# Heads in pairs through scores and values in the stick-breaking attention of a two-block transformer kernel

## The reference, cut to what matters

```python
def stick_breaking_attention(q, k, v):
    for each block of 128 queries, for each of 8 heads:
        z = einsum('bhqd,bhkd->bhqk', q_blk, k) * dh ** -0.5        # dh = 64
        earlier = key_pos < query_pos
        log_keep = where(earlier, log_sigmoid(-z), 0)
        log_stick = cumsum(log_keep, axis=3, reverse=True) - log_keep
        w = where(earlier, exp(log_sigmoid(z) + log_stick), 0)
        out = einsum('bhqk,bhkd->bhqd', w, v)
```

## Time and profile before

| | us |
|---|---|
| median of 3 executions | 2090.99 |
| lowest, highest | 2090.92, 2093.43 |
| the profiled execution, its own time | 2092.2 |
| its span, first to last instruction | 2090.4 |

### The profile page before, as it was taken

The page is one execution under the profiler, slowest core; times in us unless marked ns, Lnnn a source line. Parts: engine busy times, 40 slices in busy tenths (PEclk is TensorE's granted clock), DMA queues, the critical chain, the costliest instruction groups (busy, mean ns, idle before and its releaser), DMA issues.

```text
span 2090.4 us, 28150 instructions
## 1 busy us (share of the span) xinstructions
PE 2043.1 (98%) x11092; PEld 1720.4 (82%) x11092; DVE 1374.6 (66%) x2469; ACT 1103.8 (53%) x1722; POOL 25.9 (1%) x51
## 2 busy tenths in 40 slices
PE   7999999998989999999999999999999999999998
PEld 5988899987767788888897888888888897788886
DVE  4445566656785557655696888656765697788653
ACT  4344455445444445654645666544655645666542
POOL 0000000000000000000000000000000000000000
PEclk9999999999999999999999999999999999999999
DMA  9785576664355856655533357554756533357551
GB/s 338 249 292 197 186 262 198 211 220 158 104 162 190 262 172 196 217 179 204 193 123 120 121 195 237 182 181 151 239 174 211 186 129 121 121 181 244 185 181 46
DMA packets 281763, 392.94 MB, mean 188 GB/s; under 512 B 9580, under 2 KB 175900, under 8 KB 281504
## 3 DMA queue, kind: packets, MB, share of 16 engines
q1 hardware_dynamic: 277472, 379.62, 55.4%
q0 software_dynamic: 3184, 9.04, 1.3%
q10 hardware_dynamic: 976, 2.49, 0.3%
HBM read 390.06 MB, written 1.05 MB: 187 GB/s over the span
## 4 chain that ended last, share of the span: by engine, by line
PE 64%; DVE 7%; issue 3%; ACT 3%; DMA 0%; POOL 0%; DVEq 0%; ACTq 0%; POOLq 0%
PE bank L815 17%; PE bank L817 17%; PE bank L816 17%; PE bank L779 9%; DVE junk L2633 2%; DVE wlo L1974 2%; PE bank L940 1%; DVE wlo L1969 1%; PE bank L863 1%; ACT whi L1387 1%; DVE tm L2789 0%; DVE stats L2044 0%; DVE x L2205 0%; ACT whi L1382 0%; ACT junk L1442 0%
## 5 line engine op out<-in xcount | busy, mean ns | idle before, releaser
L1969 DVE TENSOR_TENSOR wlo<-raw,whi 128x1024 fp32r<-128x1024 f32 x360 | 434.1, 1223 | 319.4 <-ACT whi L1382 317.8
L1382 ACT ACTIVATE whi<-raw 128x1024 fp32r<-128x1024 f32 x360 | 375.1, 1057 | 410.3 <-PE bank L817 211.1
L815 PE MATMUL bank<-whi,xTh 128*128 128x512 f32 (+1 forms) x1344 | 530.1, 394 | 6.9 <-issue 2.6
L817 PE MATMUL bank<-whi,xTl 128*128 128x512 f32 (+1 forms) x1344 | 521.3, 388 | 0.0
L816 PE MATMUL bank<-wlo,xTh 128*128 128x512 f32 (+1 forms) x1344 | 520.9, 388 | 0.0
L1974 DVE SCALAR_TENSOR_TENSOR wlo<-raw,cols,whi 128x512 fp32r<-128x512 f32 (+2 forms) x608 | 407.0, 721 | 134.0 <-ACT whi L1387 130.3
L1387 ACT ACTIVATE whi<-raw,cols 128x512 fp32r<-128x512 f32 (+2 forms) x608 | 385.6, 696 | 146.0 <-PE bank L817 107.3
L815 PEld LDWEIGHTS bank<-whi,xTh 128*128 128x128 f32 x1344 | 253.3, 188 | 62.0 <-issue 7.2
L817 PEld LDWEIGHTS bank<-whi,xTl 128*128 128x128 f32 x1344 | 252.9, 188 | 52.8
L816 PEld LDWEIGHTS bank<-wlo,xTh 128*128 128x128 f32 x1344 | 253.4, 189 | 48.7
L779 PE MATMUL bank<-xTh,whi 128*128 128x256 f32 x696 | 198.1, 285 | 0.2 <-DVE wlo L1969 0.2
(11 more groups left out here) (360 smaller groups left out, 2500.8 us busy)
## 6 DMA issues: line engine op xcount, KB each, us to landing
raw<-in_w_in SPq DMA_DIRECT2D x68, 1024.0 KB, 5.2
raw<-in_ffn_w_in SPq DMA_DIRECT2D x132, 512.0 KB, 6.1
raw<-in_ffn_w_gate SPq DMA_DIRECT2D x88, 512.0 KB, 4.2
raw<-in_ffn_w_up SPq DMA_DIRECT2D x88, 512.0 KB, 5.2
raw<-in_ffn_w_down SPq DMA_DIRECT2D x40, 1024.0 KB, 5.0
raw<-in_w_mod SPq DMA_DIRECT2D x36, 1024.0 KB, 6.6
raw<-in_ffn_w_out SPq DMA_DIRECT2D x30, 1024.0 KB, 5.1
raw<-in_w_out SPq DMA_DIRECT2D x12, 1024.0 KB, 5.0
```

Of the source, the lines that this page charges most:

```text
L815: e.matmul(o, hi[:, kc, sl], wh[:, c], start=at == 0 and k == 0, stop=False)
L817: ins = e.matmul(o, lo[:, kc, sl], wh[:, c], start=False, stop=fin)
L1382: e.activation(wh, raw, ACT.Copy).then_inc(m.whi_done, 1)
L1969: e.tensor_tensor(wl, raw, wh.bitcast(F32), ALU.subtract).then_inc(m.wlo_done, 1)
```

## The change

Scores and values take two heads at a time. `scores(p)` issues the four score matmuls of heads 2p and 2p+1, alternating between the row halves, into two banks, then the masks of both; `values(p)` issues the four value matmuls of the pair, alternating between the column halves. On PE the scores of a pair come in the even steps 0, 2, 4, 6 and the values of a pair in the odd steps 3, 5, 7, 9; `sticks` stays one head per step. ACT and DVE keep their order of one head per step. `ex` gets a third buffer, and head h uses buffer h mod 3. ACT's wait before a new head's absolute value is counted in pairs of values. The bank tables are not touched.

```diff
--- before.py
+++ after.py
@@ -660,7 +660,7 @@
         self.kT, o = self.at(o, "kT", [128, 4, 256])
         self.sv, o = self.at(o, "sv", [128, 2, 512])
         self.spl, o = self.at(o, "spl", [128, 2, 384])
-        self.ex, o = self.at(o, "ex", [128, 2, 384])
+        self.ex, o = self.at(o, "ex", [128, 3, 384])
         self.lam, o = self.at(o, "lam", [128, 8])
         self.la, o = self.at(self.b1_at, "la", [128, 2, 256])
         self.l1, o = self.at(o, "l1", [128, 2, 256])
@@ -1191,19 +1191,22 @@
         ins.then_inc(full, 1)
         step = [0]
 
-        def values(h):
-            hp, off, r = h // 2, (h % 2) * 64, h % 2
-            pr = slice(off, off + 64)
-            self.evacuated("sc", l, h)
-            if h % 4 == 0:
-                self.bank("bo", l, h // 4)
-                if h == 0:
+        def values(p):
+
+            pair = (2 * p, 2 * p + 1)
+            for h in pair:
+                self.evacuated("sc", l, h)
+            if p % 2 == 0:
+                self.bank("bo", l, p // 2)
+                if p == 0:
                     self.evacuated("sv", l, 1)
-            b = self.t.bank["bo", l, h // 4][0]
-            bank, cs, hc = m.psum[b], (hp % 2) * 256, slice(h * 64, h * 64 + 64)
-            self.mm(bank[pr, cs:cs + 256], m.sv[:, 0, hc], m.ex[:, r, 0:256], h % 4 < 2, False)
-            ins = self.mm(bank[pr, cs + 128:cs + 256], m.sv[:, 1, hc], m.ex[:, r, 256:384], False, h % 4 >= 2)
-            ins.then_inc(m.full[b] if h % 4 == 3 else m.value_mm, 1)
+            b = self.t.bank["bo", l, p // 2][0]
+            bank, cs = m.psum[b], (p % 2) * 256
+            for i, o, x in ((0, slice(cs, cs + 256), slice(0, 256)), (1, slice(cs + 128, cs + 256), slice(256, 384))):
+                for h in pair:
+                    pr = slice(h % 2 * 64, h % 2 * 64 + 64)
+                    ins = self.mm(bank[pr, o], m.sv[:, i, h * 64:h * 64 + 64], m.ex[:, h % 3, x], p % 2 == 0 and i == 0, p % 2 == 1 and i == 1)
+            ins.then_inc(m.full[b] if p % 2 else m.value_mm, 1)
 
         def sticks(h):
             r = h % 2
@@ -1214,26 +1217,28 @@
             self.mm(bank[:, 128:256], NO, m.spl[:, r, 256:384], False, False)
             self.mm(bank[:, 256:384], NL, m.spl[:, r, 256:384], False, True).then_inc(m.stick_mm, 1)
 
-        def scores(h):
-            hp, off = h // 2, (h % 2) * 64
-            pr = slice(off, off + 64)
-            if h == 0:
+        def scores(p):
+
+            if p == 0:
                 self.evacuated("sk", l, 1)
-            bank, full = self.bank("sc", l, h)
-            self.mm(bank[:, 0:256], m.kT[pr, hp, 0:128], m.qT[pr, hp, 0:256], True, False)
-            self.mm(bank[:, 256:384], m.kT[pr, hp, 128:256], m.qT[pr, hp, 128:256], False, False)
-            self.mm(bank[:, 0:128], m.ident[:, :], m.stk[:, 0:128], False, False)
-            self.mm(bank[:, 256:384], m.ident[:, :], m.stk[:, 0:128], False, False).then_inc(full, 1)
+            banks = [self.bank("sc", l, 2 * p + r) for r in range(2)]
+            for o, k, q in ((slice(0, 256), slice(0, 128), slice(0, 256)), (slice(256, 384), slice(128, 256), slice(128, 256))):
+                for r in range(2):
+                    pr = slice(64 * r, 64 * r + 64)
+                    self.mm(banks[r][0][:, o], m.kT[pr, p, k], m.qT[pr, p, q], o.start == 0, False)
+            for bank, full in banks:
+                self.mm(bank[:, 0:128], m.ident[:, :], m.stk[:, 0:128], False, False)
+                self.mm(bank[:, 256:384], m.ident[:, :], m.stk[:, 0:128], False, False).then_inc(full, 1)
 
         def each():
             n = step[0]
             step[0] += 1
-            if 2 <= n < 10:
-                values(n - 2)
+            if n % 2 and 3 <= n < 10:
+                values((n - 3) // 2)
             if 1 <= n < 9:
                 sticks(n - 1)
-            if n < 8:
-                scores(n)
+            if n % 2 == 0 and n < 8:
+                scores(n // 2)
 
         def decays():
             e.wait_ge(m.la_done, l + 1)
@@ -1831,15 +1836,15 @@
         def sticks(h):
             e.wait_ge(m.stick_mm, 8 * l + h + 1)
             b, n = self.t.bank["sc", l, h]
-            e.activation(m.ex[:, h % 2, :], m.psum[b][:, 0:384], ACT.Exp).then_inc(m.free[b], 1)
+            e.activation(m.ex[:, h % 3, :], m.psum[b][:, 0:384], ACT.Exp).then_inc(m.free[b], 1)
 
         def scores(h):
             bank, _ = self.filled("sc", l, h)
-            x = m.ex[:, h % 2, :]
-            if h == 5:
+            x = m.ex[:, h % 3, :]
+            if h in (5, 6):
                 self.filled("bo", l, 0)
-            elif h >= 2:
-                e.wait_ge(m.value_mm, 6 * l + h - 1 - (h - 2 >= 4))
+            elif h >= 3:
+                e.wait_ge(m.value_mm, 2 * l + (1 if h < 5 else 2))
             e.activation(x, bank[:, 0:384], ACT.Abs).then_inc(m.act, 1)
             self.own()
             e.activation(x, x, ACT.Exp, scale=-1.0).then_inc(m.act, 1)
@@ -2679,7 +2684,7 @@
             e.wait_ge(m.ln_done, 8 * l + h + 1)
             if h >= 2:
                 e.wait_ge(m.stick_mm, 8 * l + h - 1)
-            e.scalar_tensor_tensor(out=m.spl[:, h % 2, :], in0=bank[:, 0:384], scalar=0.0, in1=m.ex[:, h % 2, :],
+            e.scalar_tensor_tensor(out=m.spl[:, h % 2, :], in0=bank[:, 0:384], scalar=0.0, in1=m.ex[:, h % 3, :],
                                    op0=ALU.max, op1=ALU.add).then_inc(m.spl_done, 1)
 
         def each():
```

## The result

The changed kernel takes 2078.39 us (median of 4, 2076.09 to 2081.99) beside 2090.95 (2089.15 to 2093.43) for the kernel before: ratio 0.9942, 95% interval 0.993 to 0.9955. That is 12.6 us faster, inside the range 2077.0 to 2088.0. The forecast of 2082.6 gave 8.4 of the 12.6. The profiled execution took 2076.09, its span is 2074.2 instead of 2090.4.

A forecast was written before the change was run, and what follows sets the result against it. PE, busy for 98% of the span, was taken to bound the kernel. Saving 4.5 us per mixer up to softplus 5, 9.0 for both, gave 2083.2 or 2082.0 by scale, middle 2082.6 us; range 2077 to 2088.

The forecast's parts named there:

- Overlap of the halves: PE's pairs on opposite array halves stream together: scores 0.85 us, values 0.81; the rival without overlap, 2087.8 us, had chance 0.09.
- The rival with 0.05: Only scores overlap; the two pairs of values lose 0.65 us each, giving 2085.2 us; chance 0.05.
- Step 0: Scores 0 and 1 put about 0.5 us more before the first stall, which shrinks from 3.49 to 3.0; no cost.
- Step 1: After sticks 0 at low clock, the sub comes earlier; sticks 1 start at about 1124.55 instead of 1126.72.
- the clock does not fall: Rival: clock stays up in first stalls, 2.75 us less a mixer; one 2079.9 us, both 2077.1; chance 0.17.
- Steps 2 to 5: From sticks 1 on, steps of 6.62, 5.51 and 8.14 us, then softplus 5 at 1148.16, 4.5 us earlier.
- Steps 6 and 7: DVE's distances from softplus 5 stay fixed: softplus 6 after 7.01 us, sticks 7 after 14.11; PE early at sticks 6 by 0.4.
- the new stall: PE waits 2.7 us for DVE in front of sticks 7; all that PE saves in steps 6 and 7 goes there.
- The clock behind it: Granted clock after sticks 7 stays 1.00; rival: it falls, 3.3 us a mixer; one 2085.9 (chance 0.13), both 2089.2 (0.07).
- The stall of 2.18 us that stood as harmless: Stall at 610.99 us, followed by a clock of 1.00; taken as a length that did not bring the clock down.
- Sum: 4.5 us saved per mixer, 9.0 for both mixers.
- The midpoint between two scales: 2082.6 us, the middle between 2083.2 (from the profiled execution's 2092.2) and 2082.0 (in the scale of the median 2090.99).

The follow-up runs named there:

- e6: Changed kernel with ACT's and DVE's work on the decays moved behind the scores of head 1: 2072.23 us, ratio 0.9908 to the kernel before.
- e8: Kernel before with one edit on PE, head 1's scores issued in step 0 behind head 0's, unpaired: 2082.10 us, ratio 0.9957.
- e5: Changed kernel with DVE's softplus ahead of the tap in steps 6 and 7, step 7's last two chunk states after softplus: 2070.89 us, ratio 0.99.
- e1: Changed kernel with one head's matmuls issued before the other's within each pair, no alternation: 2077.23 us, ratio 0.9936 to the kernel before.
- e3: Changed kernel with only values in pairs, scores and their step as in the kernel before: 2084.41 us, ratio 0.997 to the kernel before.
- e4: Kernel before with the third buffer of ex and ACT's wait moved back one head, nothing paired: 2090.59 us, ratio 0.9996.
- r_after: The changed kernel measured again, unedited, beside the kernel before: 2078.87 us, ratio 0.9938.

## Why the prediction was right, step by step

- **Overlap of the halves**: right. 0.85 and 0.80 for pairs, forecast 0.85 and 0.81. The chunk states pointed the right way, although their two groups lie on different row halves, so that they were no pure case of shared rows; the values' pair is one. The rival with 0.05, which the Trainium skill's rule on row groups ("TensorE: Matmul & The Clock Gate", Part 3, "The mechanism") stood beside, is refuted by the values' row.
- **Step 0 costs nothing**: right; the stall shrank by 0.44, forecast 0.5, and sticks 0 stayed tied to the chain on ACT, 7.83 us behind the first scores in both kernels. e6 showed that it is that chain.
- **Step 1, the term that was mis-sized**: sticks 1 "at about 1124.55", 6.95 after sticks 0. It was 5.26. The path was right, the low clock was taken to last as before, 6.5 us, and lasted 3.3: about 1.4 us. Another 0.27 is that sticks 0 took 1.73 us to the start of a product, where 2.00, their distance to scores, was taken. (The step's own terms add up to 1124.47, not 1124.55.) This is 1.7 of the 2.2 us that softplus 5 came early in each mixer. The rival "the clock does not fall" had the right direction and did not happen; that the stretch could be shorter was on no list. Whether the change made it shorter stays open (e8), so up to 1.4 us of each mixer's gain may be luck; without it the distances give 10.6 us for both mixers, nearer to the 9.0.
- **Steps 2 to 5**: 23.1 us between sticks 1 and softplus 5, forecast 23.6. Sticks 1 and 3 took 0.97 to the next start instead of 1.08 and the masks 0.92 instead of 0.94, which is half of it; the subs took 0.2 less in sum and the loop on ACT 0.14 less, and sticks 2 took 0.98 instead of 0.90. The forecast had one figure for all sticks in front of scores. Sticks 5 follow a product as well but start 0.06 us after their softplus ends, and took 1.07; sticks 1 and 3, whose softplus had ended 0.57 and 1.71 us before, took 0.97. So what comes before them does not explain the difference alone.
- **Steps 6 and 7, the new stall**: right. 7.03 and 14.13 forecast as 7.01 and 14.11, idle 0.37 and 2.57 forecast as 0.4 and 2.7. e5 shows the cause: without taps and states in front of the softplus both are gone.
- **The clock behind it**: it stayed up in this profile, as forecast, but e6's one fall in eight such stalls shows that the chance given to the rival was deserved. Its price, half of 6.5 us, was too high; the fall cost 1.6. The stall of 2.18 us that stood as harmless was no safe bound: in three of thirteen profiles (e1, e3, e6) the same stall was followed by 3.4 us at 0.50.
- **Sum**: 4.5 per mixer forecast, 6.7 and 6.8 measured between two profiles, 12.6 us between medians instead of 9.0. So the mechanism was right and the sum about 30% too small, mostly through the low clock of step 1. The midpoint between two scales was 0.6 us above before's median less the sum.

## What to carry to other kernels

When work is taken from the bounding engine, follow the other engines' fixed chains to see where the saving stops: here everything behind softplus 5 was swallowed by 14 us of DVE work, and two changes of order on DVE and ACT were worth nearly as much (10.3 us) as the pairing of matmuls (12.6). Put work in front of a stall rather than behind it: e8 gained 8 us by moving one head's scores there, part of it because the clock stayed up once. Two float32 operations on opposite halves of the array cost the time of one when they stand in one group, in whatever order.

## What the runs showed of the hardware that was not expected

- PE overlapped passes on different halves across four passes issued in between (e1: 0.86 and 0.81 us for pairs, as with alternation).
- The granted clock after nearly equal stalls differs: behind 2.84 or 2.85 us it fell for 6.8 us (before), for 3.4 (e4) and not at all (e3); behind 2.6 us it fell once (e6) and did not in seven other mixers (after, r_after, e1 and e6's second). Behind 2.18 us near 611 us it fell for 3.4 us in three of thirteen profiles.
- Behind one and the same stall of 3.9 us in the first block the low stretch was 6.8 us in seven profiles and 3.4 in six. The three falls of before ahead of the first mixer account for about 2 of the 2.7 us between the two profiles compared here.
